# Modulation vectors by product and row sum on VectorE, in place of products summed by matmuls

## The reference, cut to what matters

```python
def modulate(h, shift, scale):
    return h * (1.0 + scale[:, None, :]) + shift[:, None, :]

c_act = jax.nn.silu(c)
mod = c_act @ w_ada[l] + b_ada[l]
sh_m, sc_m, gt_m, sh_f, sc_f, gt_f = jnp.split(mod, 6, axis=-1)
h = modulate(rms_norm_2(x, g_mix[l]), sh_m, sc_m)
...
x = x + gt_m[:, None, :] * mixed
h2 = modulate(rms_norm_2(x, g_ffn[l]), sh_f, sc_f)
...
x = x + gt_f[:, None, :] * y
```

## Time and profile before

| | |
|---|---|
| median of 3 runs | 998.99 us (998.06 to 999.19) |
| the profiled execution: its own time | 998.53 us |
| its span, first to last instruction | 996.4 us |
| mean granted TensorE clock | 0.997 of full |
| loads | 194.19 MB, mean 195 GB/s |
| lines of the chain that ended last | PE L493 24%, L494 23%, L499 22%; DVE L1349 2%; ACT L891 2% |

### The profile page before, as it was taken

How to read it: one execution, slowest core, us unless ns; L and a number is a source line. 1 busy time by engine, 2 the same in 40 slices (tenths; PEclk the granted TensorE clock), 3 DMA queues, 4 the chain that set the end, 5 groups by cost and what they waited for, 6 DMA issues and landing times.

```text
span 996.4 us, 18905 instructions
## 1 busy us (share of the span) xinstructions
PE 967.1 (97%) x7999; PEld 930.4 (93%) x7999; DVE 718.6 (72%) x1270; ACT 539.3 (54%) x837; POOL 17.4 (2%) x48
## 2 busy tenths in 40 slices
PE   6989999999999999999999999999999999999997
PEld 5978999999998988899999998898999999999996
DVE  5965787877647877698867888646654878788753
ACT  6635564445346456665444545546755556656642
POOL 0000000000000000000000000000220000000000
PEclk9999999999999999999999999999999999999999
DMA  7433467676753743358775883553333544554531
GB/s 285 182 127 136 160 244 264 233 262 245 275 212 127 277 147 111 144 176 320 263 254 197 343 303 132 211 172 126 127 134 131 207 165 169 173 199 179 192 148 43
DMA packets 28307, 194.19 MB, mean 195 GB/s; under 512 B 3264, under 2 KB 3520, under 8 KB 5312
## 3 DMA queue, kind: packets, MB, share of 16 engines
q1 hardware_dynamic: 28224, 192.99, 53.2%
HBM read 191.93 MB, written 1.05 MB: 194 GB/s over the span
## 4 chain that ended last, share of the span: by engine, by line
PE 85%; DVE 7%; ACT 5%; issue 2%; DMA 1%; SPq 1%; POOL 0%; DVEq 0%; ACTq 0%
PE bank L493 24%; PE bank L494 23%; PE bank L499 22%; DVE s_wlo L1349 2%; PE bank L631 2%; PE bank L657 2%; ACT s_whi L891 2%; PE bank L554 2%; PE bank L548 1%; PE bank L549 1%; PE bank L513 1%; PE bank L520 1%; PE bank L514 1%; DMA s_raw<-in_wa 1%; PE bank L641 1%
## 5 line engine op out<-in xcount | busy, mean ns | idle before, releaser
L1349 DVE TENSOR_TENSOR s_wlo<-s_raw,s_whi 128x512 fp32r<-128x512 f32 (+1 forms) x364 | 371.2, 1061 | 137.9 <-ACT s_whi L891 137.6
L891 ACT ACTIVATE s_whi<-s_raw 128x1024 fp32r<-128x1024 f32 (+2 forms) x233 | 305.0, 1335 | 214.1 <-PE bank L499 200.1
L493 PE MATMUL bank<-s_hh,s_whi 128*128 128x256 f32 x1400 | 394.9, 282 | 0.5 <-DVE s_hl L1440 0.3
L494 PE MATMUL bank<-s_hl,s_whi 128*128 128x256 f32 x1400 | 388.2, 277 | 0.0
L499 PE MATMUL bank<-s_hh,s_wlo 128*128 128x256 f32 x1383 | 383.4, 277 | 0.0
L493 PEld LDWEIGHTS bank<-s_hh,s_whi 128*128 128x128 f32 x1400 | 263.4, 188 | 6.9 <-issue 5.3
L494 PEld LDWEIGHTS bank<-s_hl,s_whi 128*128 128x128 f32 x1400 | 263.3, 188 | 0.1
L499 PEld LDWEIGHTS bank<-s_hh,s_wlo 128*128 128x128 f32 x1383 | 259.9, 188 | 0.0
L493 PE MATMUL bank<-s_ph,s_whi 128*128 128x256 f32 x528 | 146.7, 278 | 0.0
L494 PE MATMUL bank<-s_pl,s_whi 128*128 128x256 f32 x528 | 145.9, 276 | 0.0
L499 PE MATMUL bank<-s_ph,s_wlo 128*128 128x256 f32 x516 | 142.6, 276 | 0.0
(11 more groups left out here) (239 smaller groups left out, 1301.5 us busy)
## 6 DMA issues: line engine op xcount, KB each, us to landing
s_raw<-in_gu SPq DMA_DIRECT2D x44, 1024.0 KB, 4.9
s_raw<-in_dn SPq DMA_DIRECT2D x33, 1024.0 KB, 4.9
s_raw<-in_wada SPq DMA_DIRECT2D x24, 1024.0 KB, 5.2
s_raw<-in_up SPq DMA_DIRECT2D x22, 1024.0 KB, 4.8
s_raw<-in_wo SPq DMA_DIRECT2D x8, 1024.0 KB, 4.8
s_raw<-in_win_g SPq DMA_DIRECT2D x8, 1024.0 KB, 4.9
s_raw<-in_wkv_v SPq DMA_DIRECT2D x4, 1024.0 KB, 5.7
s_raw<-in_wkv_k SPq DMA_DIRECT2D x4, 1024.0 KB, 4.8
```

The costliest lines, as they stand in the source:

```text
L493: e.matmul(out, hi, xh[:, k, :], start=first, stop=False, skip_group_check=True)
L494: e.matmul(out, hi, xl[:, k, :], start=False, stop=False, skip_group_check=True)
L891: e.activation(whi[w % SPLIT][:, at], raw[p % RAW][:, at], ACT.Copy).then_inc(S.hi.tick((w, c0)), 1)
L1349: e.tensor_tensor(wlo[s][:, at], raw[p % RAW][:, at], whi[s][:, at].bitcast(F32), ALU.subtract).then_inc(S.lo.tick((i, j), (i, "all")), 1)
```

## The change

The modulation weight is stored transposed: output columns on the partitions, the summed dimension (1024) along the row. A piece then holds two blocks of 128 outputs. `c` is loaded already repeated on all 128 partitions (512 KB) into the first half of `adacc`, once its earlier contents are used up, and its silu is taken over 128 x 1024. `ada_product` issues two products with a sum along the row, each of which writes one column of `modv`; the elementwise product goes back over the raw weights. `ada_bias` adds the bias in place. TensorE's three sums are gone: one has no successor (in the gate/up loop), two are replaced by `keep_warm` calls of 11 and 13. The columns of `c` in `cols` and the tile `cact` go.

```diff
 for _name, _n in (("pre0", 8), ("inv", 1), ("pre1", 8), ("post0", 8), ("post1", 8), ("fpre0", 8), ("fpre1", 8), ("fpost0", 8),
-                  ("fpost1", 8), ("kvsrc", 8), ("gq", 3), ("gkv", 2), ("gmix", 8), ("gffn", 8), ("gfin", 8), ("c", 8),
+                  ("fpost1", 8), ("kvsrc", 8), ("gq", 3), ("gkv", 2), ("gmix", 8), ("gffn", 8), ("gfin", 8),
                   ("bada", 48), ("cw0", 44), ("cw1", 44), ("cw2", 44), ("cb", 44)):
...
         modv = sb("modv", [P, 48])
-        cact = sb("cact", [P, 8])
         gs2 = sb("gs2", [P, 16])
...
             bias2 = sb("bias2", [P, 8, T], F32, scope)
-        gates, gates2 = yb, adacc
+        gates, gates2, cact = yb, adacc, adacc[:, 0:D]
         squares_yg, new_yg, terms, new_term = tmps[:, 0:2, :], tmps[:, 2:4, :], tmps[:, 4:6, :], sqb[2]
...
         S.x_in = [signal(f"x_in{i}", 16) for i in range(4)]
-        S.relb_in, S.relm_in = signal("relb_in", 16), signal("relm_in", 16)
+        S.relb_in, S.relm_in, S.c_in = signal("relb_in", 16), signal("relm_in", 16), signal("c_in", 16)
         S.raw_in = [signal(f"raw_in{i}", 16) for i in range(RAW)]
...
                     q.wait_ge(S.attn, ("o0", "values", 3))
+                    q.wait_ge(S.rot, ("q", 1))
+                    e.dma_start(cact[:, :], a["c"]).then_inc(S.c_in.tick("c"), 16)
                     e.dma_start(bias1[:, :, :], a["relb"]).then_inc(S.relb_in.tick("relb"), 16)
...
                 m.then_inc(S.sums.tick(s), 1)
-
-            def ada_sums(g, b):
-                out = take(b, S.mod, g)
-                bank_of["ada", g] = b
-                q.wait_ge(S.ada, ("group", g))
-                for j in range(16):
-                    m = e.matmul(out[:, j:j + 64], adacc[:, j * P:(j + 1) * P], ones[:, 0:64], start=True, stop=True)
-                m.then_inc(S.sums.tick(("ada", g)), 1)
...
                         sums({0: "x1", 1: "x3"}[layer], 0)
-                    if layer == 1 and n == 32:
-                        ada_sums(1, 0)
                 lead_dn(d, layer)
...
             feed_forward(0, "h1", sqb[3])
-            ada_sums(0, 6)
+            keep_warm(11, 6)
...
                 m.then_inc(S.sums.tick(of), 1)
-            ada_sums(2, 4)
+            keep_warm(13, 4)
...
                     if layer == 0 and n == 0:
-                        e.activation(cact[:, :], col("c", 0, 8), ACT.Silu).then_inc(S.act_tmp.tick("cact"), 1)
+                        q.wait_ge(S.c_in, "c")
+                        e.activation(cact[:, :], cact[:, :], ACT.Silu).then_inc(S.act_tmp.tick("cact"), 1)
                     if n >= 1:
...
-                g, kc = at // 8, at % 8
                 q.wait_ge(S.raw_in[i % RAW], i)
                 q.wait_ge(S.act_tmp, "cact")
-                src = raw[i % RAW][:, :]
-                if kc == 0:
-                    if g > 0:
-                        q.wait_ge(S.sums, ("ada", g - 1))
-                    else:
-                        q.wait_ge(S.attn, ("o0", "values", 3))
-                        q.wait_ge(S.rot, ("q", 1))
-                    m = e.tensor_scalar(adacc[:, :], src, cact[:, 0:1], None, ALU.mult)
-                else:
-                    q.wait_latest(S.ada)
-                    m = e.scalar_tensor_tensor(out=adacc[:, :], in0=src, scalar=cact[:, kc:kc + 1], in1=adacc[:, :],
-                                               op0=ALU.mult, op1=ALU.add)
-                m.then_inc(S.ada.tick(i, ("group", g)), 1)
+                for half in range(2):
+                    j = 2 * at + half
+                    src = raw[i % RAW][:, half * D:(half + 1) * D]
+                    m = e.tensor_tensor_reduce(out=src, in0=src, in1=cact[:, :], scale=1.0, scalar=0.0, op0=ALU.mult,
+                                               op1=ALU.add, accum_out=modv[:, j:j + 1])
+                m.then_inc(S.ada.tick(i, ("group", at // 8)), 1)
             def ada_bias(g):
-                bank = banks[bank_of["ada", g]]
-                q.wait_ge(S.sums, ("ada", g))
-                e.tensor_tensor(modv[:, g * 16:(g + 1) * 16], bank[:, 0:16], col("bada", g * 16, 16), ALU.add).then_inc(
-                    S.mod.tick(g), 1)
+                q.wait_ge(S.ada, ("group", g))
+                e.tensor_tensor(modv[:, g * 16:(g + 1) * 16], modv[:, g * 16:(g + 1) * 16], col("bada", g * 16, 16),
+                                ALU.add).then_inc(S.mod.tick(g), 1)
...
                  gkv=f["mla_g_kv"][0], gmix=f["g_mix_2"][0], gffn=f["g_ffn_2"][0], gfin=f["g_final_2"],
-                 c=f["c_2"][0], bada=f["b_ada_2"][0], cw0=f["w_conv_2"][0, 0], cw1=f["w_conv_2"][0, 1],
+                 bada=f["b_ada_2"][0], cw0=f["w_conv_2"][0, 0], cw1=f["w_conv_2"][0, 1],
                  cw2=f["w_conv_2"][0, 2], cb=f["b_conv_2"][0], inv=np.tile(inv.astype(np.float32), 4))
...
     o["dn2"] = _pieces(_lead(_tiles(f["w_down_2"][0]), 2))
-    o["wada"] = _pieces(f["w_ada_2"][0].reshape(8, P, 3, 16, P).transpose(2, 0, 3, 1, 4))
+    o["wada"] = f["w_ada_2"][0].T.reshape(24, 2, P, D).transpose(0, 2, 1, 3).reshape(1, -1)
+    o["c"] = np.broadcast_to(f["c_2"], (P, D))
     return {k: np.ascontiguousarray(v) for k, v in o.items()}
```

## The result

The changed kernel takes 1002.23 us (median of 6, 1001.57 to 1003.94), the kernel before, beside it on the same chip, 998.94 (997.94 to 999.19): a ratio of 1.0033, 95% interval 1.0023 to 1.0044. It is 3.3 us slower where 4.3 less had been forecast. The profiled execution took 1001.57 us around a span of 999.5.

The account below looks back on a forecast made before the run. TensorE's own list of matmuls, plus short waits for a norm between layers, was taken to bound the kernel. Terms -3.48 - 1.16 + 0.3 = -4.3 us took 998.99 to 994.7 us, range 993.0 to 997.2.

Parts of the forecast that it names:

- part 5: Load of c on SyncE's queue, 512 KB more: cost 0 (bounds 0 and 2.3 us); later tiles' 64-byte shift: 0, 0.5 either way.
- Part 1: Second modulation group's sum removed from layer 1's gate/up loop: next product starts sooner, gain 3.48 us.
- Part 2: Boundary after layer 0: warming replaces sums, the next product no longer waits for the bias addition's chain; gain 1.16 us.
- Part 3: Boundary before the second block: warming replaces sums, TensorE's idle time grows from 0.82 to 1.43 us; gain 0.
- Rival B: Clock falls at the third boundary after 1.43 us idle, losing 1.7 us: 996.4 us; chance 0.12.
- Part 4: VectorE's products with sum: 1.22 us each, 2.30 a piece; loss 0.3 us at the start of layer 0's gate/up loop.
- Rival A: VectorE's product with sum runs at half speed, 4.6 us a piece: slower, 1003.4 us; chance 0.12.
- The sum: Whole kernel: -3.48 - 1.16 + 0.3 = -4.3 us, about 994.7 us.
- the forecast's own range: Whole kernel: 993.7 to 996.0 us, before widening for the spread of runs; the forecast's chance 0.70.

Follow-up runs that it names:

- experiment 1: Changed kernel with 64 unused bytes per partition put back where the small tile was, against the kernel before: ratio 0.9945, 994.8 us.
- experiment 2: Kernel before, modulation untouched, with gs2 put into the 64-byte gap so later tiles move down 64 bytes, against the kernel before: ratio 1.0075.
- experiment 11: Kernel of experiment 1 with sixteen matmuls of the removed size on constant tiles put back in layer 1's loop, against the kernel before: ratio 0.9980.
- experiment 12: Changed kernel with the 64 bytes back and every product with sum issued twice, against the kernel before: ratio 1.0127.
- experiment 3: Changed kernel with 64 unused bytes behind the small and scratch tiles, just ahead of the stages' tiles, against the kernel before: ratio 0.9937, 993.0 us.
- experiment 5: Changed kernel with 64 unused bytes ahead of the first tile, so weights and streamed tiles move together, against the kernel before: ratio 1.0030.
- the changed kernels of the table: Changed kernel with 0, 32, 64, 128, 192, 320 unused bytes, or split weights moved up 64: ratios 1.0033, 1.0012, 0.9945, 1.0048, 1.0016, 0.9946, 1.0198.

## Why the prediction was wrong, point by point

- **The step that failed is the last sentence of part 5:** "Dropping c's columns and the small tile shifts later tiles by 64 bytes; I know no row that prices this: 0, with 0.5 either way". Its size is 8.8 us by experiment 1, 7.5 by experiment 2: matmuls whose streamed tile had moved against the weights went from 112.8 to 118.0 ns each. The 0.5 had no row behind it. A term without a row needs a bound from what it can reach: 1,596 matmuls stream `s_ph` and `s_pl` back to back, so each nanosecond of their pace is 1.6 us. The code had its own sign: two gaps of 960 and 64 unused bytes around `hh` and `hl`, which do nothing but place tiles.
- **Part 1** held, and was undersized: -3.48 forecast, 4.2 in the traces. The removed matmuls themselves are 3.5 to 3.6 of it by experiment 11. The other 0.6 to 0.7 is pace: in the kernel before, the matmuls behind the sums run at 0.118 us up to 536, and where the sums are gone they run at 0.113.
- **Part 2** held: -1.16 forecast, -1.3 in the traces, with the releaser, the undelayed low part and the 0.46 as foretold.
- **Part 3** held: 0 forecast, 0.0 measured, the gap 1.44 against 1.43. Rival B, a falling clock, didn't come: around the gap of 1.44 us the granted clock stays at 1.00 and nothing is lost up to 700 us. In experiment 12, with waits of 3.75 and 1.49 us at this boundary, it did fall.
- **Part 4** held: 1.22 us forecast, 1221 ns; 2.30 a piece, 2.29; a loss of 0.3 at 142 us, 0.25. Rival A falls for this operation; its price was too low besides, 18 us where 8.7 were worked out (experiment 12). The Trainium skill's page "Vector Engine (DVE) Microarchitecture Reference", section 7 (Points that are easy to get wrong), says of one family of two-source forms that two SBUF sources not in bf16 halve its throughput. The trace shows no such halving for the form that the change uses, 1221 ns for 1024 columns; whether the page's family takes it in, the page doesn't say.
- **Part 5, the load of c:** 0 forecast; no stage shows a cost beyond the placing, though the bias behind it took 10.0 us, not 9.1. It wasn't tried by itself.
- **The sum** without the failed term is -4.3 against -5.5 (4.1 to 6.8) in experiment 1. Of the 1.2 between them, 0.7 is part 1's and 0.1 part 2's; the rest is smaller than what single executions differ by: at 131 us, before any modulation work, experiment 1's profiled execution was 2.4 us behind that of the kernel before, and experiment 3's 0.6 ahead. (The upper end of the forecast's own range, 996.0, adds up to 995.8 from its terms; nothing hangs on it.)

## What to carry to other kernels

Look at every change of a tile's size, or a dropped tile, as a move of all that is allocated behind it; if matmuls stream a moved tile in a full stretch, compare their pace from start to start before and after, and when it differs, put the bytes back before judging the change. Bound a term that has no row by the number of instructions that it touches, not by a feeling of its smallness. An engine's spare time in a long stretch says little of the chain at its end: what it is behind by comes due there.

## What the runs showed of the hardware that was not expected

The pace of back-to-back matmuls (128 x 128 weights, 256 columns, one load of weights for each) depends on the distance in SBUF between the streamed tile and the weights: of seven distances two, 256 bytes apart, gave 112.8 and 112.7 ns, the other five 116.9 to 119.2. It is no matter of absolute address (experiment 5), and the modulation on VectorE was the same in all the changed kernels of the table. The Trainium skill, "SBUF — State Buffer", section "SBUF: two separate sides", says that TensorE never waits for another engine's access. The traces agree: 278 ns a matmul on `s_ph` with VectorE's new products (experiment 1) as without them. My reading of the rest, which no run shows, is that TensorE's own two reads hold each other up; the mechanism stays open.

There is also a slower pace at good distances. In the kernel before, behind the sums, `s_hh` is streamed at 0.118 us a matmul from 518 to 536 us:

```profile
519.67 0.28 PE L493 MATMUL bank<-s_hh,s_whi 128*128 128x256 f32 x1
519.79 0.28 PE L494 MATMUL bank<-s_hl,s_whi 128*128 128x256 f32 x1
519.91 0.28 PE L499 MATMUL bank<-s_hh,s_wlo 128*128 128x256 f32 x1
520.02 0.28 PE L493 MATMUL bank<-s_hh,s_whi 128*128 128x256 f32 x1
```

It ends at 536 with a tile whose third matmul is issued in two halves of 128 columns (L496, L497), and the pace is 0.113 again. Experiment 2's kernel, with the same sums, shows it at the same matmuls; experiment 11's, with sums on other tiles, does not. Other stretches of it end at such a pair of halves too, in the kernel before at 871 us, in experiment 1's at 824 and 914. It may be a matter of how the two reads fall in time, but what sets it wasn't tried. Such a stretch of 17 us costs some 0.7 us, and it comes at different places in different kernels, so a difference of that size between two of them need not be the edit's.
